# A two-layer decoder trunk on one core: three reordered places in layer 0, and blank TensorE products around the inner norms

## What is computed

```python
z = x @ w_in[i]
q, k, v, u, g_attn, g_ssm = jnp.split(z, splits, axis=-1)
a_out = sliding_window_attention(q, k, v, attn_sinks[i], rel_bias)
s_out = s5_mixer(u, ...)          # complex diagonal recurrence, gelu, GLU
merged = (jax.nn.sigmoid(g_attn) * (a_out @ w_branch_attn[i])
          + jax.nn.sigmoid(g_ssm) * (s_out @ w_branch_ssm[i]))
x = layer_norm(DEEPNORM_ALPHA * x + merged @ w_out[i], ln1_g[i], ln1_b[i])
ffn = swiglu(x, ...) if i % 2 == 0 else moe_swiglu(x, ...)   # dense, then top 2 of 8 experts
ple = jax.nn.sigmoid(x @ ple_w_gate[i]) * (p[i] @ ple_w_proj[i])
x = layer_norm(DEEPNORM_ALPHA * x + ffn + ple, ln2_g[i], ln2_b[i])
```

## Time and profile before

| | us |
|---|---|
| median of 3 runs | 1611.16 |
| lowest and highest run | 1610.75, 1612.85 |
| the profiled execution: device time | 1609.16 |
| its span, from the first to the last event in the trace | 1607.3 |
| TensorE busy in that span | 1570.6 |
| VectorE (DVE) busy | 1354.6 |
| ScalarE (ACT) busy | 999.9 |
| GpSimd (POOL) busy | 149.8 |

### The profile page before, as it was taken

One profiled execution on the slowest core, in us unless ns is written; L12 is line 12 of the kernel. 1 busy time (PEld: TensorE's weight loads), 2 busy tenths in 40 slices (PEclk: granted clock), 3 DMA queues, 4 the chain that ended last, 5 costly groups with the idle time before them and its releaser, 6 DMA issues.

```text
span 1607.3 us, 24068 instructions
## 1 busy us (share of the span) xinstructions
PE 1570.6 (98%) x9028; PEld 1332.7 (83%) x9028; DVE 1354.6 (84%) x1300; ACT 999.9 (62%) x913; POOL 149.8 (9%) x157
## 2 busy tenths in 40 slices
PE   8999999999999999999999999999999999999996
PEld 6889799999899978888888888888888888888884
DVE  8797856655687788999998999998999998999998
ACT  7345444334546437776777777777677677767763
POOL 2000139940300000000000000000000000000000
PEclk9999999999999999999999999999999999999998
DMA  7535855554444568999999999999999999999993
GB/s 225 162 107 183 301 180 192 185 183 132 130 132 148 200 230 297 360 372 359 361 369 334 351 369 370 352 366 334 351 371 360 354 377 332 345 377 364 360 361 124
DMA packets 169448, 456.55 MB, mean 284 GB/s; under 512 B 7638, under 2 KB 60919, under 8 KB 168872
## 3 DMA queue, kind: packets, MB, share of 16 engines
q1 hardware_dynamic: 168472, 450.87, 78.1%
q0 software_dynamic: 768, 4.75, 0.8%
q10 hardware_dynamic: 144, 0.05, 0.0%
HBM read 453.02 MB, written 2.62 MB: 283 GB/s over the span
## 4 chain that ended last, share of the span: by engine, by line
PE 86%; DVE 8%; issue 3%; DMA 1%; ACT 1%; SPq 0%; DVEq 0%; ACTq 0%
PE psum L735 20%; PE psum L737 20%; PE psum L736 20%; PE psum L742 6%; PE psum L744 6%; PE psum L743 6%; PE psum L845 4%; DVE wl L466 2%; PE psum L1199 1%; PE psum L871 1%; ACT wh L460 1%; PE psum L802 1%; DMA ring<-in_w_pg 1%; DVE hid L2190 1%; DMA ring<-in_w_in 1%
## 5 line engine op out<-in xcount | busy, mean ns | idle before, releaser
L466 DVE TENSOR_TENSOR wl<-ring,wh 128x2048 fp32r<-128x2048 f32 x269 | 609.3, 2287 | 67.0 <-ACT wh L460 63.2
L460 ACT ACTIVATE wh<-ring 128x2048 fp32r<-128x2048 f32 x307 | 581.7, 1920 | 126.3 <-PE psum L737 78.4
L736 PE MATMUL psum<-wl,xgh 128*128 128x512 f32 x896 | 349.2, 390 | 0.0
L735 PE MATMUL psum<-wh,xgh 128*128 128x512 f32 x704 | 282.0, 401 | 1.0 <-DVE xgl L2174 0.5
L737 PE MATMUL psum<-wh,xgl 128*128 128x512 f32 x704 | 274.9, 390 | 0.0
L736 PEld LDWEIGHTS psum<-wl,xgh 128*128 128x128 f32 x896 | 168.5, 188 | 32.4
L735 PE MATMUL psum<-wh,hidh 128*128 128x512 f32 x440 | 172.7, 393 | 3.7 <-DVE wl L466 2.8
L736 PE MATMUL psum<-wl,hidh 128*128 128x512 f32 x448 | 174.4, 389 | 0.0
L737 PE MATMUL psum<-wh,hidl 128*128 128x512 f32 x440 | 171.4, 390 | 0.0
L466 DVE TENSOR_TENSOR wl<-ring,wh_spare 128x2048 fp32r<-128x2048 f32 x72 | 164.5, 2284 | 3.0 <-ACT wh_spare L460 3.0
L735 PEld LDWEIGHTS psum<-wh,xgh 128*128 128x128 f32 x704 | 132.2, 188 | 33.6 <-DVE wl L466 5.5
(11 more groups left out here) (435 smaller groups left out, 2769.5 us busy)
## 6 DMA issues: line engine op xcount, KB each, us to landing
ring<-in_moe_gu SPq DMA_DIRECT2D x224, 1024.0 KB, 7.2
ring<-in_moe_dn SPq DMA_DIRECT2D x112, 1024.0 KB, 7.3
ring<-in_w_in SPq DMA_DIRECT2D x25, 1024.0 KB, 5.4
ring<-in_w_gu SPq DMA_DIRECT2D x22, 1024.0 KB, 5.1
ring<-in_w_dn SPq DMA_DIRECT2D x11, 1024.0 KB, 4.9
ring<-in_w_out SPq DMA_DIRECT2D x8, 1024.0 KB, 6.2
ring<-in_w_pg SPq DMA_DIRECT2D x8, 1024.0 KB, 5.2
ring<-in_w_ba SPq DMA_DIRECT2D x4, 1024.0 KB, 5.1
```

Of the source, the lines that this page charges most:

```text
L460: eng.activation(parts(u)[0], ring[:, ring_slot(u), :], ACT.Copy).then_inc(hi_ready, 1)
L466: eng.tensor_tensor(lo, ring[:, ring_slot(u), :], hi.bitcast(F32), ALU.subtract).then_inc(lo_ready, 1)
L735: pe.matmul(dst, ah, bh, start=first, stop=False, skip_group_check=True)
L736: pe.matmul(dst, ah, bl, start=False, stop=False, skip_group_check=True)
```

## The change

Five edits. `raw` is loaded behind unit 1, in front of `cst`, where it was loaded behind unit 0. In layer 0 TensorE makes the local maps before it turns the values. ACT copies the values before the keys, in both layers. In layer 0 units 14 and 15 are parted where layer 1 parts them: `early_hi(15)` in front of the hi part of the gated output, `early_lo(14)` in front of `gated`, `early_lo(15)` in front of `gated_lo`. And `turn` first calls `stay_awake`: once the block's variance is there, three plain float32 products of the identity with 256 columns of `cst` go into the first PSUM bank that the block's transposes will overwrite. `turn` is called for two blocks at each of the three inner norms, so 18 blank products are added.

```diff
+AWAKE = 3
...
                     if u == 1:
-                        sp.dma_start(raw.rearrange("p a b c -> p (a b c)"), bc_in[0]).then_inc(raw_dma, 16)
                         sp.dma_start(relb_sb[0:BUCKETS + 1], relb).then_inc(table_dma, 16)
                         sp.dma_start(hot_sb[0:BUCKETS + 1], hot_in).then_inc(table_dma, 16)
                     if u == 2:
+                        sp.dma_start(raw.rearrange("p a b c -> p (a b c)"), bc_in[0]).then_inc(raw_dma, 16)
                         small_loads()
...
-                    turn_values(), local_products(0), input_states(0), scores(0)
+                    local_products(0), turn_values(), input_states(0), scores(0)
...
+                def stay_awake(n, b, times):
+
+                    pe.wait_ge(var_ready, NB * n + b + 1)
+                    for _ in range(times):
+                        pe.matmul(bank[OUT_BANKS[2 * b]][:, 0:SEQ], ident, cst[:, 0:SEQ], start=True, stop=True)
+
                 def turn(src, b):
 
+                    stay_awake(1 if src is xa else 2 * l, b, AWAKE)
                     pe.wait_ge(ln_ready, b + 1 + (NB if src is xa else 2 * NB * l))
...
+                act.activation(vt.rearrange("p a b -> p (a b)"), group(4)[:, 1, :], ACT.Copy).then_inc(v_ready, 1)
                 for kv in range(2):
                     for q in (0, HD):
                         ins = act.activation(kT[q:q + HD, kv, :], group(4)[kv * HD:(kv + 1) * HD, 0, :], ACT.Copy)
                 ins.then_inc(qk_ready, 1)
-                act.activation(vt.rearrange("p a b -> p (a b)"), group(4)[:, 1, :], ACT.Copy).then_inc(v_ready, 1)
...
-                if l == 1:
-                    early_hi(15)
+                early_hi(15)
                 for b in range(2):
                     act.wait_ge(s_ready, 2 * l + b + 1)
                     act.activation(gsh[:, 2 * b:2 * b + 2, :], sT[:, 2 * b:2 * b + 2, :], ACT.Copy, scale=0.25).then_inc(s_hi, 1)
-                if l == 0:
-                    early_hi(15)
...
-                if l == 1:
-                    early_lo(14), gated(0), gated(1), early_lo(15)
-                else:
-                    gated(0), gated(1), early_lo(14)
+                early_lo(14), gated(0), gated(1), early_lo(15)
                 dve.wait_ge(s_ready, 2 * (l + 1))
                 gated_lo(0), gated_lo(1)
-                if l == 0:
-                    early_lo(15)
```

## The result

| | changed kernel | kernel before, same rounds |
|---|---|---|
| median, us | 1603.79 | 1610.77 |
| lowest and highest run | 1602.89, 1603.94 (5 runs) | 1608.92, 1612.85 (5 runs) |
| the profiled execution: device time | 1603.79 | 1609.16 |
| its span | 1602.0 | 1607.3 |
| TensorE busy in that span | 1575.4 | 1570.6 |

The ratio is 0.9946, with a 95% interval of 0.9933 to 0.996. The change makes the kernel faster by 0.4 to 0.7%. So the direction was right and the size too small.

The account below looks back on a forecast made before the run. TensorE was taken to bound the kernel, so only its waits and slow clock counted. Terms 1.5 + 2.1 + 0.7 + 1.5 + 1.0 - 1.05 = 5.75 us gave 1603.4 profiled, 1605.4 us as median, range 1602.8 to 1608.2.

Parts of the forecast that it names:

- The load: Start of the kernel: loading `raw` behind unit 1 shortens TensorE's 2.09 us wait for unit 1; 1.5 us saved, bounds 0 to 2.09.
- unit 1 comes no earlier: Rival at the start: the load's term is 0, giving 1606.9 us; chance 0.08.
- The values: Layer 0, local maps before turned values: TensorE's 2.13 us wait goes; 2.1 us saved, at least 1.9, at most 2.13.
- The parted units: Layer 0's gated output: TensorE's wait for unit 15's lo part goes; 0.7 us saved, between 0.3 and 0.75.
- a later fixed point: Rival: a landing or DVE in layer 0 eats the early gains; 1607.6 (half) or 1609.7 us (all); chance 0.06.
- The clock at the mixer's norms: Blank products keep the clock at 1.00 through both mixer's norms: 1.5 us saved in layer 0, 1.0 in layer 1.
- Cost of the blank products: 0 at the mixer's norms, where both sets fit TensorE's idle time; 1.05 us between the layers, bounds 0.9 and 1.33.
- The forecast wait of 0.2 to 0.4 us in front of the transposes: Sign in the later profile: transposes with blank products in front wait 0.2 to 0.4 us for DVE; none between the layers.
- I keep that distance: Step from profiled execution to median: the 2.0 us between them is kept, turning 1603.4 into 1605.4 us.
- The first rival: Unprofiled runs had one more slow stretch, between the layers; blank products remove 1.6 us more, giving 1603.8 us; chance 0.12.

Follow-up runs that it names:

- the first group: First of three groups of four experiments, sharing one chip and runs of the kernel before, whose median there was 1611.15 us (24 runs).

## Why the prediction was right in its parts and too small as a whole

Against the profiled execution the sum was good: 1603.4 was forecast, 1603.79 came. By its terms:

- *The load*: 1.5 forecast, 1.74 measured, all of the wait but 0.38. `raw` had its cover: DVE's first read is at 20.37 us where it was 20.34. The rival by which unit 1 comes no earlier fell.
- *The values*: 2.1 forecast, 2.35 in the lead at the scan, a little over the forecast's upper end of 2.13. The scan's own wait only shrank, 8.46 us in the earlier trace rows to 4.29 now.
- *The parted units*: 0.7 forecast, 0.67 measured at the gated output. But 0.5 of the lead was gone behind the norm of layer 0, which the small rival of a later fixed point had named in kind. The critical chain names it: the landing of the first unit of `w_pg`. SP issues that load when TensorE frees a buffer, ACT takes the hi part when it has landed, and behind ACT stands DVE's list up to the norm. Before (the piece of the chain, then ACT's row):

```profile
174.64 4.82 DMA ring<-in_w_pg
```

```profile
179.48 1.93 ACT L460 ACTIVATE wh<-ring 128x2048 fp32r<-128x2048 f32 x1 [1.20 <-DMA ring<-in_w_pg]
```

  and now:

```profile
169.96 5.24 DMA ring<-in_w_pg
```

```profile
175.23 1.93 ACT L461 ACTIVATE wh<-ring 128x2048 fp32r<-128x2048 f32 x1 [0.60 <-DMA ring<-in_w_pg]
```

  The load is issued 4.68 us earlier but takes 0.42 longer, and ACT's row leads by 4.25, just as the transposes do: they start 13.25 us behind it in both executions. That distance is 13.25 or 13.26 us in nine of the other executions too; in two it is 13.41 and 13.43, where the chain names a landing of `w_out` instead, and with five blank products 13.80. The time from issue to landing differs between executions, also of one kernel: 5.24 and 4.86 us in the two of the changed kernel, 5.81 with the load alone. So the last landing in front of the norm sets its time; why it takes longer in one execution than in another stays open, and I made no experiment on it.
- *The clock at the mixer's norms*: 1.5 and 1.0 forecast, 1.56 and 0.96 measured (the leads above).
- *Cost of the blank products*: 0 at the norms holds, and 1.05 between the layers measured 1.16. By the runs at a clock of 0.997 of the first group, the kernel with the blank products alone is 0.8 us above before (means 1607.6 and 1606.8). The forecast wait of 0.2 to 0.4 us in front of the transposes was 0.54 for the first block and too small to be shown for the second. The first is longer since the idle piece grew: TensorE's last product of `w_pp` leads by 4.68 us, DVE's normed rows by 4.25, by the landing above.

**The step that failed** is the one behind the sum: "I keep that distance", 2.0 us between the profiled execution and the median. It isn't an offset of the profiler. It is slow stretches, and the change removes them with the rest. The kernel before took 1605.9 to 1607.3 us in its five runs at 0.997 (mean 1606.6), and 1611.2 to 1611.4 in the median of those two groups; so some 4.7 us of its median run were slow stretches, where my terms had 2.5. Its profiled execution, 2.6 us above 1606.6, had two short ones, and 1.56 + 0.96 = 2.5. Take the changes that don't concern the clock, 1.74 + 2.35 + 0.67 - 1.16 = 3.6, of which up to 0.8 was given back later (0.5 at that landing, the rest in small pieces of layer 1 that I didn't trace), from 1606.6, and the changed kernel should take 1603.0 to 1603.8 in each run; it took 1602.9 to 1604.2 in the ten that there are. Of the 7.5 us between these medians of before, some 1611.3, and 1603.8, then, 2.8 are waits, less what the blank products cost, and 4.7 clock. And the clock's part isn't the work of the blank products alone: the drop behind the wait for unit 1 went with the earlier load.

The first rival, "one more slow stretch", had the mechanism and the time, 1603.8, against 1603.79 measured. That it fits to a hundredth is luck: it added one drop of 1.6 us between the layers, where some 2.2 us more than my terms were lost, over four places. I gave it 0.12. The trace had spoken for it in two ways: three runs that spread by 2.1 us, and pauses between the layers much like those at the norms. I read one execution's windows as a property of the kernel. The Trainium skill, page "TensorE: Matmul & The Clock Gate", section "Part 1: The HAM clock gate", says that the monitor is free-running and that the number of cold products at a kernel's start differs from run to run. The steps in the runs above and the table of places show such a difference inside the kernel, too. Even this rival missed the place that costs most: behind the wait for unit 1 the drop took 3.2 and 4.7 us from two executions, because the products there follow each other without a pause. So the load edit saves its wait and a possible drop behind it.

What stays open: how often each place drops in the median run. The single edits moved the median by at most 3.1 us, with intervals nearly as wide, and the profiles are too few for a rate.

## What to carry to other kernels

Before a forecast is set against a median, read the mean clock of every run, not of the profiled one alone: a spread that follows the clock is work that a change can remove, and the kernel's runs at the highest clock show what is left when all of it is gone. Treat each idle piece of TensorE between dense products as a place that may drop, also one at the start that a load causes. Fill such a piece with blank products only where another engine sets its end, and size each set by its own gap: a set in front of transposes that wait for nobody costs its full length.

## What the chip showed that I had not expected

TensorE's wait of 1.6 to 2.3 us for a load, 16 us into the program, was followed in three executions of five (waits of 2.05, 2.18 and 2.25 us, but not 1.63 and 2.09) by 6.8 to 10.3 us at the 1.2 GHz level, longer than the 3.4 us stretches of the earlier trace rows; with a wait of at most 0.76 us none of nine had it. And blank products proved sure where idle pieces were not: none of 21 covered places dropped, 12 of 21 uncovered ones did, although TensorE still has 0.2 to 0.6 us of idle time around its transposes, and 1.57 us in front of the first product of layer 1.
